# The last experts' rows reach their tokens by products with a gate matrix; the channel norm runs in two token groups

## The reference, cut to what matters

```python
for layer in range(2):
    h = rms_norm(x, norm_mix[layer])
    if layer == 0:
        x = x + band_attention(h) @ w_o
    else:                               # conv_module
        a, g = split(h @ w_pw1 + b_pw1)
        u = a * sigmoid(g)
        dw = depthwise_conv(u, w_dw) + b_dw          # 31 taps
        x = x + silu(layer_norm(dw, ln_g, ln_b)) @ w_pw2 + b_pw2
    x = x + hier_moe(rms_norm(x, norm_ffn[layer]))
y = rms_norm(x, norm_final)

def hier_moe(xt):            # 4 groups of 8 experts: best group, its two best experts
    gates = (n, 32), two values other than 0 in each row
    hid = silu(xt @ w_gate[e]) * (xt @ w_up[e])      # 256 columns, for each expert e
    return sum over e of (gates[:, e] * hid) @ w_down[e]
```

## Time and profile before

| | before |
|---|---|
| median of 3 runs | 1279.36 us (1279.34 to 1279.62) |
| the profiled execution | 1279.65 us, span 1278.0 us |
| PE busy | 1063.3 us (83%) |
| DVE busy | 493.3 us (39%) |
| ACT busy | 289.6 us (23%) |
| POOL busy | 272.5 us (21%) |
| mean granted clock of TensorE | 0.922 of full |

### The profile page before, as it was taken

One profiled execution on the slowest core, in us unless ns is written; L12 is line 12 of the kernel. 1 busy time (PEld: TensorE's weight loads), 2 busy tenths in 40 slices (PEclk: granted clock), 3 DMA queues, 4 the chain that ended last, 5 costly groups with the idle time before them and its releaser, 6 DMA issues.

```text
span 1278.0 us, 14398 instructions
## 1 busy us (share of the span) xinstructions
PE 1063.3 (83%) x5242; PEld 609.9 (48%) x5242; DVE 493.3 (39%) x1066; ACT 289.6 (23%) x616; POOL 272.5 (21%) x289
## 2 busy tenths in 40 slices
PE   6999999998995978887854999987985978788870
PEld 5777777774543333332323777743543323333320
DVE  3234444344356111110116699993455111111116
ACT  3233232333111101000003455553111100000002
POOL 3000000000003111111042488850003111101033
PEclk9999999999995999988885999998996989999895
DMA  8953322302706999999955922100027999999963
GB/s 278 389 172 109 109 97 78 106 22 105 296 36 227 408 419 420 420 420 421 414 174 132 367 61 66 33 25 0 34 101 286 413 421 421 421 420 420 379 255 131
DMA packets 107791, 303.67 MB, mean 238 GB/s; under 512 B 18248, under 2 KB 65480, under 8 KB 82745
## 3 DMA queue, kind: packets, MB, share of 16 engines
q1 hardware_dynamic: 85481, 254.74, 51.4%
q0 software_dynamic: 22256, 48.22, 10.4%
HBM read 278.34 MB, written 57.12 MB: 262 GB/s over the span
## 4 chain that ended last, share of the span: by engine, by line
PE 58%; DMA 21%; DVE 10%; issue 8%; ACT 2%; SPq 1%; POOL 0%; DVEq 0%; POOLq 0%
DMA ring<-in_w_up 16%; PE bank L1200 12%; PE bank L522 10%; PE bank L421 7%; PE bank L1217 6%; PE bank L549 4%; DVE bank L1680 2%; PE bank L1478 2%; PE bank L572 2%; PE bank L1190 2%; PE bank L588 2%; PE bank L613 2%; PE bank L346 2%; DMA work<-in_w_pw 1%; PE bank L954 1%
## 5 line engine op out<-in xcount | busy, mean ns | idle before, releaser
L1200 PE MATMUL bank<-ring,work 128*64 128x512 f32 x704 | 179.1, 667 | 34.9 <-DMA ring<-in_w_up 33.1
L1217 PE MATMUL bank<-ring,work 128*64 128x512 f32 x528 | 124.9, 616 | 36.7 <-DVE work L1236 22.4
L1478 PE MATMUL bank<-arena,work 128*128 128x288 f32 x512 | 129.2, 415 | 8.2 <-issue 3.2
L1200 PEld LDWEIGHTS bank<-ring,work 128*64 128x64 f32 x704 | 61.4, 153 | 150.3 <-issue 147.8
L522 PE MATMUL bank<-arena,ring 128*128 128x288 f32 x512 | 131.9, 412 | 0.0
L1232 DVE TENSOR_TENSOR work<-work,bank 128x256 f32<-128x256 f32 x33 | 13.9, 421 | 292.2 <-ACT work L1228 292.2
L1478 PEld LDWEIGHTS bank<-arena,work 128*128 128x128 f32 x512 | 99.0, 195 | 38.0 <-issue 8.3
L1627 POOL TENSOR_TENSOR ring<-ring 128x606 f32<-128x606 f32 x76 | 103.8, 1365 | 55.8 <-ACT ring L1576 46.2
L522 PEld LDWEIGHTS bank<-arena,ring 128*128 128x128 f32 x512 | 94.9, 190 | 32.6 <-issue 7.9
L421 PE MATMUL bank<-ring,arena 128*128 128x512 f32 x224 | 100.9, 604 | 6.6 <-ACT arena L1611 6.6
L1680 DVE SCALAR_TENSOR_TENSOR bank<-work,ring,bank 128x606 f32<-128x606 f32 x129 | 98.8, 844 | 0.0
(11 more groups left out here) (256 smaller groups left out, 1293.9 us busy)
## 6 DMA issues: line engine op xcount, KB each, us to landing
ring<-in_w_down SPq DMA_DIRECT2D x32, 2048.0 KB, 24.1
ring<-in_w_gate SPq DMA_DIRECT2D x22, 2048.0 KB, 22.0
ring<-in_w_up SPq DMA_DIRECT2D x22, 2048.0 KB, 28.9
arena<-in_w_gate SPq DMA_DIRECT2D x10, 2048.0 KB, 23.0
arena<-in_w_up SPq DMA_DIRECT2D x10, 2048.0 KB, 31.1
ring<-in_w_qkv SPq DMA_DIRECT2D x24, 512.0 KB, 6.0
y_sorted<-gain POOLq DMA_DIRECT2D x8, 1536.0 KB, 5.7
work<-in_w_pw SPq DMA_DIRECT2D x16, 512.0 KB, 5.1
```

The lines of the kernel that those rows point to most:

```text
L1200: mm = nc.tensor.matmul(bank[2 + s][rr, :], xte[s][:, c, rr], wgu[g][:, :, e, c, :], start=c == 0, stop=c == C - 1)
L1217: mm = nc.tensor.matmul(bank[5 + h][rr, :], hts[:, c, rr], wdn[s][:, e, c, h * HALF:(h + 1) * HALF], start=c == 0, stop=c == FC - 1)
L1478: mm = nc.tensor.matmul(bank[banks[h][w]][:, 0:GT], wp[s][:, w, c, :], xt[:, c, h * GT:(h + 1) * GT], start=c == 0, stop=c == C - 1)
```

## The change

Pairs 0 to 14 are scattered to `y_sorted` as before. After pair 14 GpSimd gathers all ten `y_at` tiles at once; a token whose slot is in pair 15 or in an overflow pair reads a row of zeros (`ZERO_ROW`). Pair 15 and the overflow pairs are no longer stored. DVE builds, for each, `token_at`: 128 tokens by 128 slots for each of the ten (k, tile) combinations, the gate value where the token has that slot, else 0 (`find_tokens`). PE turns and adds the two k of each tile by products with the identity (`turn_places`), DVE copies the result (`spread`, `spread_more`), and PE multiplies it with `ysb` straight to the tokens' rows (`spread_pe`); DVE adds the ten half tiles from PSUM to `x` (`spread_add`). The gathered rows are combined before the overflow pairs run, and an overflow pair's rows are spread inside its turn of the loop, ahead of pair 15's. ACT copies both halves of pair 15's output, and both halves of every overflow copy that DVE shared before.

In the norm ahead of the convolution ACT copies both halves of each turned tile; the last two tiles' turns stand inside the first GLU products. `conv_first` waits for all gathers, for the spread products and for `combined` before its three groups of loads; `wp`'s two buffers change places and so do `xe` and `xte`. The norm's `combined` now counts two a tile.

The channel norm runs in two token groups, of 256 and 320 columns: variance, root, reciprocal, scaling and swish. `project_pe` waits for the second group only at its third tile.

`place`, `at_slot`, `ocmp` and a part of `diag` share memory with `token_at`. The router computes `early_slot` another way, and `spread_rel`, each slot's place relative to pair 15 and the overflow pairs.

```diff
-        SLOTS = (EXPERTS + OVER) * CAP
+        ZERO_ROW = EXPERTS * CAP
+        SLOTS = ZERO_ROW + P
...
-        EARLY_TILES = 4 * C * FE // D - TILES
-        y_at = [[ring[:, 1, (TILES * k + j) * D:(TILES * k + j + 1) * D] for j in range(TILES)] for k in range(2)]
+        RING_TILES = 4 * C * FE // D
+        FAR_TAIL = 2 * TILES * D - (2 * TILES - RING_TILES) * D
+        y_tiles = [ring[:, 1, n * D:(n + 1) * D] for n in range(RING_TILES)] + [
+            arena[:, FAR_TAIL + n * D:FAR_TAIL + (n + 1) * D] for n in range(2 * TILES - RING_TILES)]
+        y_at = [y_tiles[k * TILES:(k + 1) * TILES] for k in range(2)]
+        spread_more = ring[:, 1, 5 * C * FE:5 * C * FE + TOKENS]
+        SPREAD_BANKS = ((0, 1), (2, 3), (4, 7), (5, 6))
...
-        EARLY_PAIRS = EPAIRS - 2
+        EARLY_PAIRS = EPAIRS - 1
...
+            if n == 2:
+                for j, turn in ((0, None), (1, 0), (2, 1), (None, 2), (3, None), (4, 3), (None, 4)):
+                    if j is not None:
+                        norm_act(act, steps, n, j)
+                    if turn is not None:
+                        turn_act(act, n, turn)
+                        turn_copy(act, nc.scalar.copy, n, turn, 1, turn_ev_d)
+                return
...
+            if n > 0:
+                for j, norm in ((0, None), (1, 0), (2, 1), (3, None), (4, 2), (None, 3), (None, 4)):
+                    if j is not None:
+                        spread_add(dve, base, j, KJ * (n // 2 - 1))
+                    if norm is not None:
+                        norm_dve(dve, steps, n, norm)
+                return
             for j in range(TILES + 2):
-                if n > 0 and j < TILES:
-                    combine_dve(dve, steps, n // 2 - 1, j)
...
+            for local in range(EARLY_PAIRS):
...
-                if local == EARLY_PAIRS:
-                    pool.wait_ge(further_known, 2 * (l + 1))
-                    pool.wait_ge(base.y_out[0], 16 * (EPAIRS // 2) * (l + 1))
-                    pool.wait_ge(base.y_out[1], 16 * (EPAIRS // 2) * (l + 1))
-                    for j in range(TILES):
-                        for k in range(2):
-                            if early(j, k):
-                                y_rows_in(pool, j, k, early_slot)
...
+            pool.wait_ge(further_known, 2 * (l + 1))
+            pool.wait_ge(far_scattered, 16 * (2 * TILES - FAR_FIRST) * (l + 1))
             for s in range(2):
-                pool.wait_ge(base.y_out[s], 16 * (EPAIRS // 2) * (l + 1) + 16)
-            pool.wait_ge(extra_end, l + 1)
+                pool.wait_ge(base.y_out[s], outs_before(s, l + 1, 0))
             for j in range(TILES):
-                pool.wait_ge(gathered[j], landed(j, l + 1, late=False))
                 for k in range(2):
-                    y_rows_in(pool, j, k, late_slot if early(j, k) else slot)
+                    pool.indirect_dma_start(y_at[k][j][0:rows[j], :], None, y_sorted,
+                                            bass.IndirectOffsetOnAxis(early_slot[0:rows[j], k, j:j + 1], 0),
+                                            bounds_check=SLOTS - 1, oob_is_err=False).then_inc(gathered[j], 16)
+
+        def outs_before(s, l, local):
+
+            per_layer = len(range(s, EARLY_PAIRS, 2))
+            return 16 * (1 + per_layer * l + local // 2)
 
         def combine_dve(dve, steps, l, j):
             r = rows[j]
-            dve.wait_ge(gathered[j], landed(j, l + 1))
-            steps.done(nc.vector.scalar_tensor_tensor(x[0:r, j, :], y_at[0][j][0:r, :], gate_w[0:r, 0, j:j + 1],
-                                                      x[0:r, j, :], ALU.mult, ALU.add))
-            nc.vector.scalar_tensor_tensor(x[0:r, j, :], y_at[1][j][0:r, :], gate_w[0:r, 1, j:j + 1],
-                                           x[0:r, j, :], ALU.mult, ALU.add).then_inc(combined, 1)
+            dve.wait_ge(gathered[j], 32 * (l + 1))
+            for k in range(2):
+                steps.done(nc.vector.scalar_tensor_tensor(x[0:r, j, :], y_at[k][j][0:r, :], gate_w[0:r, k, j:j + 1],
+                                                          x[0:r, j, :], ALU.mult, ALU.add))
...
+        def spread_add(dve, m, j, count):
+            r = rows[j]
+            for h in range(2):
+                dve.wait_ge(m.spread_mm, count + 2 * j + h + 1)
+                here = x[0:r, j, h * HALF:(h + 1) * HALF]
+                nc.vector.tensor_tensor(here, here, spread_out(j, h), ALU.add).then_inc(m.spread_ev, 1)
+
+        def spread_pe(pe, m, s, to_token, count):
+            for j in range(TILES):
+                if j == TILES - 1:
+                    pe.wait_ge(m.spread_ev, count + 4)
+                for h in range(2):
+                    nc.tensor.matmul(spread_out(j, h), to_token[:, j * P:j * P + rows[j]], ysb[s][:, h * HALF:(h + 1) * HALF],
+                                     start=True, stop=True).then_inc(m.spread_mm, 1)
+
+        def turn_places(j, out):
+            r = rows[j]
+            for k in range(2):
+                mm = nc.tensor.matmul(out, token_at[0:r, k * TILES + j, :], ident[0:r, 0:r], start=k == 0, stop=k == 1)
+            return mm
+
+        def turn_first_places():
+            for j in range(TILES - 1):
+                mm = turn_places(j, bank[7][:, j * P:(j + 1) * P])
+            return mm
+
+        def turn_last_places():
+            return turn_places(TILES - 1, bank[4][:, FE:FE + DEC])
+
+        def find_tokens(dve, found, n):
+            V = nc.vector
+            found(V.tensor_tensor(token_at, iota[:].unsqueeze(1).to_broadcast([P, KJ, P]),
+                                  n.unsqueeze(2).to_broadcast([P, KJ, P]), ALU.is_equal))
+            return V.tensor_tensor(token_at, token_at, gate_w[:].rearrange("p k j -> p (k j)").unsqueeze(2).to_broadcast(
+                [P, KJ, P]), ALU.mult)
...
+        def ex_down_pe(pe, m, i, s, k, loads, spreads=False):
             pe.wait_ge(m.hid, i + 1 + FREE)
+            if m is not base:
+                turn_first_places()
             for c in range(FC):
                 mm = nc.tensor.transpose(bank[4][:, c * P:(c + 1) * P], hid_pc[:, c, :], ident[:])
+            if spreads:
+                mm = turn_last_places()
             mm.then_inc(m.ht_mm, 1)
+            if spreads and m is base:
+                turn_first_places().then_inc(m.g_mm, 1)
...
-                ex_down_pe(pe, extra, i, 0, i, 2)
+                ex_down_pe(pe, extra, i, 0, i, 2, spreads=True)
+                pe.wait_ge(extra.ht_ev, i + 1)
+                pe.wait_ge(extra.y_ev_a, i + 1 + FREE)
+                spread_pe(pe, extra, 0, spread_more, KJ * i)
+                pe.wait_ge(extra.spread_ev, KJ * (i + 1))
 
             extra_turns(pe, l, further)
+            pe.wait_ge(base.g_ev, l + 1)
+            for y_ev in base.y_evs:
+                pe.wait_ge(y_ev, EPAIRS * (l + 1) + FREE)
+            spread_pe(pe, base, 1, spread, KJ * l)
...
+                ex_y_copy(act, nc.scalar.copy, base, i, s, 0, base.y_ev_a, outs_before(s, l, local))
+                if not more:
+                    ex_y_copy(act, nc.scalar.copy, base, i, s, 1, base.y_ev_d, outs_before(s, l, local))
...
+                if local == EARLY_PAIRS - 1:
+                    steps.done(find_tokens(dve, steps.done, spread_rel[:, 0, :]))
 
             turns(body, l)
+            V = nc.vector
+            V.tensor_copy(spread[:, SEQ:TOKENS], bank[4][:, FE:FE + DEC])
+            dve.wait_ge(base.g_mm, l + 1)
+            V.tensor_copy(spread[:, 0:SEQ], bank[7][:]).then_inc(base.g_ev, 1)
+            for j in range(TILES):
+                combine_dve(dve, steps, l, j)
 
             extra = extras[l]
 
             def further(i):
-                ex_turn_copy(dve, nc.vector.tensor_copy, extra, i, 0, 1, extra.xt_ev_d)
+                def found(instruction):
+                    instruction.then_inc(extra.found, 1)
+                    dve.wait_ge(extra.found, i + 1)
+
+                find_tokens(dve, found, spread_rel[:, dyn(i + 1, 1), :].rearrange("p a n -> p (a n)"))
                 ex_hid_dve(dve, extra, i, 0)
+                dve.wait_ge(extra.ht_mm, i + 1)
+                V.tensor_copy(spread_more[:, SEQ:TOKENS], bank[4][:, FE:FE + DEC])
+                V.tensor_copy(spread_more[:, 0:SEQ], bank[7][:])
                 ex_ht_dve(dve, extra, i)
-                ex_y_copy(dve, nc.vector.tensor_copy, extra, i, 0, i, 1, extra.y_ev_d)
+                for j in range(TILES):
+                    spread_add(dve, extra, j, KJ * i)
...
-            def extra_store(o):
-                sp.wait_ge(extra.y_ev_a, o + 1 + FREE)
-                sp.wait_ge(extra.y_ev_d, o + 1 + FREE)
-                sp.dma_start(rows_of(y_sorted, EPAIRS + o), ysb[0]).then_inc(extra.y_out[0], 16)
-                sp.wait_ge(extra.y_out[0], 16 * (o + 1))
-                sp.sem_inc(extra.y_free, 1)
...
-            sp.wait_ge(gathered[0], landed(0, 1))
+            sp.wait_ge(base.gu_mm, EPAIRS)
```

(44 more changed lines are left out.)

159 lines of the change are left out of this document (82 added, 77 removed).

## The result

The changed kernel took 1297.05 us (median of 4 runs, 1290.8 to 1299.93) beside 1279.49 us (1279.34 to 1282.82) for the kernel before on the same chip: 1.0124 times the time, 95% interval 1.0084 to 1.0165. It is 17.6 us slower. The forecast was 1280.7, with a range of 1274.5 to 1287. The run that was profiled is the slowest of the four, 1299.93 us with a span of 1298.2.

The account below looks back on a forecast made before the run. The page's TensorE-bound average was judged to say little; waits at three seams (end of layer 0, channel norm, end of layer 1) decide. -3.0 - 5.3 + 9.6 = +1.3 on a 1279.36 us median gave 1280.7, range 1274.5 to 1287.

Parts of the forecast that it names:

- Seam A: End of layer 0: one round of gathers replaces pair 15's scatter and a second round; -3.0 us (-1.5 to -7).
- ten from about 651 have landed by 667 and are hidden: End of layer 0: ten gathers, issued every 1.30 us, land behind other work and cost nothing.
- The overflow test on DVE: End of layer 0: DVE makes this test after real work and not in idle time; 0.5 us added.
- My steps after the first whole tile: End of layer 0: spread additions, small vectors, turn 2 and norms, with the last norm ending near 694.6.
- Seam B: Channel norm: two token groups let the first projection product start 4.95 us earlier, plus a clock gain; -5.3 us (-4.5 to -7.1).
- second term: Channel norm: less PE idle time gives the first projection products a fuller clock, worth only 0.35 us more.
- Seam C: End of layer 1, with one overflow pair: +13.2 to the first whole tile, -3.6 in the tail; +9.6 us (+6.5 to +14).
- rival 2: Slower by the end of layer 1 alone, through late gathers (some +4) or a lasting half clock; 1285.1 us, chance 0.37.
- Loop entry: End of layer 1: overflow test and entry into the overflow loop on DVE, between 0 and 1.23 us, taken as 0.7.
- the half clock that I had charged to the turns alone: End of layer 1: idle PE turns the gate matrix at 0.50 clock, 4.5 us not 2.8; down products stay 3.65.
- The rest, from the overflow's rows to the first whole tile: End of layer 1: ten spread products 8.6 us, last addition and loop end 1.0, two more products with additions 2.4.
- no change: The main forecast for the whole kernel: 1280.7 us, a difference under 0.2% (2.6 us) counting as none; chance 0.43.

Follow-up runs that it names:

- interleave: Changed kernel with tiles 3 and 4 gathered first and combined after the overflow pair, tiles 0 to 2 each just before its spread additions; 1283.27 us, ratio 1.0022.
- second profile: The changed kernel run again without any edit, as a control; 1296.09 us, ratio 1.0110 to the kernel before.
- places_early: Changed kernel with pair 15's gate matrix built by DVE after pair 8 and not after pair 14; 1296.08 us, ratio 1.0117 to the kernel before.
- combine_last: Changed kernel with DVE combining all gathered rows after the overflow pair and not before it; 1291.21 us, ratio 1.0082 to the kernel before.

## Why the prediction was wrong

**Seam A: forecast -3.0, measured +5.9 and +7.0.** The step that failed is "ten from about 651 have landed by 667 and are hidden". The gathers were issued from 653.25, 2.3 us after my start, and the rows of tile 3, for which DVE waited, were there only at 672.7. The start had to be later: the trace of the kernel before has pair 14's scatter issued at 647.40 and landed 5.8 us later, at 653.2, and my 651 left it 3.6. In the changed kernel it took 7.5. As for the landings, I had gone by the issue interval of 1.30 us and left the last gather some 4 us. The trace gives 6.9 and 8.7 us for tile 4's two, and DVE's wait up to 10.3 for tile 3's second. Ten gathers are 4.7 MB, an estimated 15 us at the 308 to 333 GB/s of the busy stretches, and the late packets come on top.

Combining ended at 677.94 for the forecast 672.1. DVE began it 3.3 us late (662.31 for 659.0, in part behind pair 15's slow up products) and then waited 2.5. In the second profile those products were fast and DVE waited for gathers three times instead, to end at 678.4: the gathers decide. The overflow test on DVE took 1.54 us where I had 0.5, and the first norm tile came 6.9 us late, which reached the last (701.64 for 694.6) unchanged. My steps after the first whole tile held: 20.8 us to the last norm's end, forecast 20.7. `interleave` shows the other half of the fault: the combining of tiles 1 and 2 need not stand ahead of the first whole tile.

The end of the norm is 4.1 us late, the seam 5.9. The other 1.8 (2.7 in the second profile) are lost behind it, where the forecast had nothing: the third block's products start 5.0 us late, at 740.13 for 735.16, and take 72.43 us for 71.54. No run here says why.

**Seam B: forecast -5.3, measured -6.1 to -7.1.** Right in mechanism: the 10.65 us from the first variance to the first projection product were forecast as 10.5. The second term, 0.35 for the clock, was too small: between the first projection product and U another 1.3 to 2.3 us are gained. The first 48 records of the projection alone give 1.8 (20.84 us for 22.67), at a granted clock of 1.00 where the earlier trace rows have 0.50.

**Seam C: forecast +9.6, measured +20.4 and +17.0.** The order was right: DVE combines before `hid`, `hid` was late, the clock was half, the tail took 13.5 us for the forecast 14.0. The sizes:
- Gathers. I had combining start at 1229.2 and allowed 1.0 us of waits beside its 13.1. The scatter was issued 1.9 us later than I had it and landed in 9.1 us instead of 7.6, so that the first gather came at 1226.83 and combining started at 1233.60, forecast 1229.2; between tiles DVE then waited 3.4 us. Combining ended at 1250.04, forecast 1243.3: +6.7. This is rival 2's "late gathers", for which I had +4.
- Loop entry: 0.99 for 0.7.
- Down products: 6.34 us for 3.65, the half clock that I had charged to the turns alone; the turns took 5.25 for 4.5. Together +3.4, in the first run; in the second the down products were at full clock.
- The rest, from the overflow's rows to the first whole tile, took 12.75 for 12.0.

These bring the first whole tile to 1281.35 for 1270.2 (6.7 + 0.3 + 3.4 + 0.75, some 11.2).

The likeliest case by my chances was "no change" (0.43); slower, which came, had 0.37. The range ended 10 us short. That was not only a matter of adding the seams up: their own upper ends (-1.5, -4.5 and +14) sum to 1287.4, and seams A and C each came out beyond theirs. Late gathers, the larger part of both, had +4 in seam C and nothing in seam A, though one cause acts in both layers.

The Trainium skill, TensorE: Matmul & The Clock Gate, Part 1, says that the number of slow products varies between runs. Here the trace agrees: the same 16 products took 6.34 us in one run of the changed kernel and 3.65 in the other. By that rule a forecast with the half clock through the down products would have been an estimated 2.7 us higher, still inside my range.

What stays open: why pair 14's scatter, issued behind the weight stream, takes 7.5 and 9.1 us to land (3.30 for pair 15's in the earlier trace rows). `places_early` excludes DVE's work beside it. In layer 0 the profiled runs gave 7.5, 4.8, 5.8 and 5.8 us (the changed kernel twice, `combine_last`, `interleave`); the short ones were issued later (648.6, 648.4 and 646.9 for 644.7), and all four landed between 652.3 and 654.2. In the one with 7.5 us the DMA engines were busy 0.07 of the time between 648 and 652, so it is a few late packets again and not full engines. The 12 us that seam C still costs in `interleave` were not reduced by any kernel here. Its rows suggest that two rounds of ten products and ten additions cost more than the store, the wait and the gathers that they replace, but no run takes one of the two rounds away. No version of the change as a whole gains anything here: the norm groups with the old gathers are the fastest (1273.8).

## What to carry to other kernels

When transfers that were spread over two stages are put into one round, price the round by its bytes at the rate that the trace shows, with the late packets on top (20.4 us here from the first issue to the last landing in layer 0), and not by its issue interval, and put first what the next stage needs first. On an engine that works in order, work that is "free" in one layer can stand ahead of a chain in another: list what is queued behind each moved block at every place where the code runs. And when one unknown (here, how late gathers land) enters two seams, let it count in both, and let the range move both together.
